# The trunk's MLP: up and down both as seven block products for eight, hidden values by way of DRAM

## The reference

```python
def mlp_sq_relu(hn, w_up, w_down):
    return jnp.square(jax.nn.relu(hn @ w_up)) @ w_down
...
        h = h + mlp_sq_relu(rmsnorm(h, norm_mlp[i]), w_up[i], w_down[i])
        gate = jax.nn.sigmoid(rmsnorm(h, norm_ple[i]) @ w_ple_gate[i])
        h = h + gate * (p[i] @ w_ple_proj[i])
```

## Time and profile before

| | us |
|---|---|
| median of 3 runs | 2668.34 |
| lowest, highest | 2668.11, 2674.18 |
| profiled execution, its own time | 2672.45 |
| its span, first to last instruction | 2670.8 |

### The profile page before, as it was taken

How to read it: one execution, slowest core, us unless ns; L and a number is a source line. 1 busy time by engine, 2 the same in 40 slices (tenths; PEclk the granted TensorE clock), 3 DMA queues, 4 the chain that set the end, 5 groups by cost and what they waited for, 6 DMA issues and landing times.

```text
span 2670.8 us, 33174 instructions
## 1 busy us (share of the span) xinstructions
PE 2598.1 (97%) x12228; PEld 2148.8 (80%) x12228; DVE 1693.7 (63%) x2448; ACT 1051.0 (39%) x1758; POOL 788.0 (30%) x671
## 2 busy tenths in 40 slices
PE   7999999899999999999999999989999999999996
PEld 6788888788888888888878888878888888888885
DVE  7667655645666766675665657664567766667555
ACT  6555433433333333334442333353333333333432
POOL 2000000023555555543120000002355554554213
PEclk9999999999999999999999999999999999999998
DMA  3000100121111111211221111012111111111121
GB/s 131 30 25 25 32 25 24 56 79 40 56 56 56 43 53 48 63 51 59 88 94 40 32 32 31 24 63 79 48 56 56 50 46 49 55 56 55 48 79 71
DMA packets 39531, 140.49 MB, mean 53 GB/s; under 512 B 4384, under 2 KB 4400, under 8 KB 39392
## 3 DMA queue, kind: packets, MB, share of 16 engines
q1 hardware_dynamic: 36448, 128.73, 15.6%
q0 software_dynamic: 2224, 7.54, 0.8%
q10 hardware_dynamic: 720, 2.36, 0.2%
HBM read 129.70 MB, written 8.91 MB: 52 GB/s over the span
## 4 chain that ended last, share of the span: by engine, by line
PE 73%; issue 16%; DVE 6%; ACT 4%; DMA 1%; DVEq 0%; POOL 0%; ACTq 0%; SPq 0%; POOLq 0%
PE gemm_ps L487 15%; PE gemm_ps L489 15%; PE gemm_ps L488 15%; PE s_ps L487 8%; PE s_ps L488 7%; PE s_ps L489 7%; PE to_ps L488 1%; PE to_ps L489 1%; PE to_ps L487 1%; PE to_ps L593 1%; ACT prob L1117 1%; DVE wlo L1462 1%; ACT whi L1031 1%; DVE prob L1584 0%; DVE h L2133 0%
## 5 line engine op out<-in xcount | busy, mean ns | idle before, releaser
L487 PE MATMUL gemm_ps<-b_hi,whi 128*128 128x512 f32 x1280 | 499.6, 390 | 0.0
L489 PE MATMUL gemm_ps<-b_hi,wlo 128*128 128x512 f32 x1280 | 498.0, 389 | 0.0
L488 PE MATMUL gemm_ps<-b_lo,whi 128*128 128x512 f32 x1280 | 497.9, 389 | 0.0
L487 PE MATMUL gemm_ps<-a_hi,whi 128*128 128x512 f32 x1024 | 424.3, 414 | 21.1 <-DVE a_lo L1471 10.8
L489 PE MATMUL gemm_ps<-a_hi,wlo 128*128 128x512 f32 x1024 | 402.6, 393 | 0.0
L488 PE MATMUL gemm_ps<-a_lo,whi 128*128 128x512 f32 x1024 | 401.3, 392 | 0.0
L1462 DVE TENSOR_TENSOR wlo<-wraw,whi 128x1024 fp32r<-128x1024 f32 x162 | 221.5, 1368 | 138.4 <-ACT whi L1031 137.8
L487 PE MATMUL s_ps<-hid_hi,whi 128*128 128x512 f32 x784 | 305.0, 389 | 0.0
L488 PE MATMUL s_ps<-hid_lo,whi 128*128 128x512 f32 x784 | 305.0, 389 | 0.0
L489 PE MATMUL s_ps<-hid_hi,wlo 128*128 128x512 f32 x784 | 305.0, 389 | 0.0
L487 PEld LDWEIGHTS gemm_ps<-b_hi,whi 128*128 128x128 f32 x1280 | 240.2, 188 | 50.8 <-issue 1.0
(11 more groups left out here) (267 smaller groups left out, 4417.4 us busy)
## 6 DMA issues: line engine op xcount, KB each, us to landing
wraw<-panels SPq DMA_DIRECT2D x162, 512.0 KB, 3.5
wraw<-pairs SPq DMA_DIRECT2D x56, 512.0 KB, 3.6
h<-x_t SPq DMA_DIRECT2D x11, 512.0 KB, 5.4
h_spill<-h POOLq DMA_DIRECT2D x8, 512.0 KB, 3.1
h<-h_spill SPq DMA_DIRECT2D x8, 512.0 KB, 4.4
out_t<-h SPq DMA_DIRECT2D x8, 512.0 KB, 2.8
h<-x_t ACTq DMA_DIRECT2D x4, 512.0 KB, 11.4
p_raw<-p_t POOLq DMA_DIRECT2D x2, 1024.0 KB, 6.0
```

What stands on the lines that cost most here:

```text
L487: nc.tensor.matmul(out, hi_w, hi_x, start=start, stop=False, skip_group_check=True)
L488: nc.tensor.matmul(out, hi_w, lo_x, start=False, stop=False, skip_group_check=True)
L489: return nc.tensor.matmul(out, lo_w, hi_x, start=False, stop=stop, skip_group_check=True)
```

## The change

The up projection is folded as well, and all of down. Each layer's MLP becomes a list of 34 turns of 7 blocks. Turns 0 to 15 are the up projection: turn n makes 256 hidden values by 1024 positions, as a 2x2 of 128x512 (a "sub", quarters B11, B12, B21, B22), each block product over 4 pieces of 128 inputs, so 12 matmuls. VectorE and ScalarE put the quarters together, scale, clamp and square them, and SP stores them in a DRAM tensor, four stores of 256 KB a turn. Turns 16 to 33 are down (`DOWN`: output pair q, first sub, number of subs): a block product over 4 subs is 12 matmuls, over 2 subs (turns 16, 17, 32, 33) 6. The subs are loaded back piece by piece, summed in place by GpSimd (4 sums a sub), split by ScalarE and VectorE, and kept for the two turns of each output group that use them; `taken_in(n, j)` says which block of which sub is split at position j of turn n.

Weights: a turn's raw pair is two loads of 512 KB (half that for two-piece turns); three of the four weight sums are made in place by GpSimd; split blocks stand in a ring of 4 places, made 3 blocks ahead (`AHEAD`). The four banks of PSUM alternate between two sets by turn. The sums u2 and p7 of down lie in zs, sumsq, zt and rstd, one pair of places for each q; before, u2 and m1 lay in zs and u3 apart. They are added to h at the end only: by GpSimd for q 0 to 2 (`tail_adds`), by VectorE for q 3.

The high parts of x for turn 0 are made while the output projection of the mixer still runs, together with the sums T1 to T4 of x on VectorE (`t_part`), and the low parts of T3 on GpSimd (`t3_lo`). The norm's matmuls before up follow block 1 of turn 0. The squares for the norm before the gate (`tail_square`, GpSimd's `tile_squares`) come after the high parts of h, the gate's next weight split and the copy of p; the norm's matmuls follow the gate's whole first panel. In an up turn VectorE has 9 steps for the quarters (5 read PSUM) and ScalarE 2 copies and 4 squares beside the 7 weight blocks; in a down turn VectorE has 7 reads of PSUM.

The diff, cut to what the text speaks of (removed lines are left out):

```diff
+SUBS = FF // (2 * P)
+UPS = SUBS
+DOWN = ([(2, 0, 2), (3, 0, 2)] +
+        [(q + 2 * h, 4 * c + 2 * h, 4) for c in range(4) for h in range(2) for q in range(2) if 4 * c + 2 * h < 14] +
+        [(2, 14, 2), (3, 14, 2)])
+TURNS = UPS + len(DOWN)
+LAST = TURNS - 1
...
+RING = 4
+AHEAD = 3
+RAMP = {(15, 2): [(0, 0)], (15, 3): [(0, 1), (0, 2)], (15, 4): [(0, 3)], (15, 5): [(0, 4), (0, 5)],
+        (15, 6): [(0, 6), (1, 0)], (16, 0): [(1, 1)], (16, 1): [(1, 2)], (16, 2): [(1, 3)], (16, 3): [(1, 4)],
+        (16, 4): [(1, 5)], (16, 5): [(1, 6)], (16, 6): [(2, 0)], (17, 0): [(2, 1)], (17, 1): [(2, 2)],
+        (17, 2): [(2, 3)], (17, 3): [(2, 4)], (17, 4): [(2, 5)], (17, 5): [(2, 6)]}
+def taken_in(n, j):
+    found = list(RAMP.get((n, j), []))
+    first = n - UPS + 1 if n % 2 else n - UPS
+    if n >= 17 and n % 2 and 4 <= first < SUBS and j:
+        found.append((first, j - 1))
+    if n >= 18 and n % 2 == 0 and 4 <= first < SUBS and j == 0:
+        found.append((first, BLOCKS - 1))
+    if n >= 17 and n % 2 and 2 <= first < SUBS and j == BLOCKS - 1:
+        found.append((first + 1, 0))
+    if n >= 18 and n % 2 == 0 and 2 <= first < SUBS and j < BLOCKS - 1:
+        found.append((first + 1, j + 1))
+    return found
...
+                def load_raw(n):
+                    if n == 0:
+                        sp.wait_ge(w_lo_ready, st["gate"])
+                    elif n == 1:
+                        sp.wait_ge(up_t3_ready, 4 * layer + 3)
+                        sp.wait_ge(up_t_ready, 16 * layer + UP_T.index(("T4", 2)) + 1)
+                    else:
+                        sp.wait_ge(blk_lo_ready, BLOCKS * (turn_of(layer, n) - 1))
...
+                def load_hidden(s, name):
...
+                    elif name == "B11":
+                        sp.wait_ge(hid_lo_ready, taken_at(layer, s - 1, X_BLOCK.index("T2")))
+                        sp.wait_ge(t_ready, t_made(layer, s - 1, "T4"))
+                    else:
+                        last = {"B12": "T3", "B22": "B22", "B21": "T4"}[name]
+                        sp.wait_ge(hid_lo_ready, taken_at(layer, s - 1, X_BLOCK.index(last)))
...
+                for n in range(UPS, TURNS):
+                    s = n - UPS + 2
+                    if n + 2 < TURNS:
+                        load_raw(n + 2)
+                    if s < SUBS:
+                        for name in ("B11", "B12", "B22", "B21"):
+                            load_hidden(s, name)
+                sp.wait_ge(blk_lo_ready, BLOCKS * turn_of(layer, LAST))
+                load_panels(st["gate"], 4 + KT)
...
+                def fold_turn(n):
+                    t, count = turn_of(layer, n), pieces_of(n)
+                    down = n >= UPS
+                    for j, (_, _, name, start) in enumerate(FOLD):
+                        out = BANKS[n % 2][name]
+                        pe.wait_ge(blk_lo_ready, BLOCKS * t + j + 1)
...
+                        if j == 0 and n >= 2:
+                            pe.wait_ge(fold_read, reads(layer, n - 1))
                         if j == 2:
+                            pe.wait_ge(fold_read if down else p_copied,
+                                       reads(layer, n) + 1 if down else 2 * (UPS * layer + n) + 1)
                         if j == 5:
+                            pe.wait_ge(fold_read if down else p_copied,
+                                       reads(layer, n) + 2 if down else 2 * (UPS * layer + n) + 2)
                         if j == 6:
+                            pe.wait_ge(fold_read, reads(layer, n) + (5 if down else 3))
+                        for i in range(count):
+                            x_hi, x_lo = input_block(n, j, i)
+                            last = product(out, blk(whi, layer, n, j)[:, i], blk(wlo, layer, n, j)[:, i], x_hi, x_lo,
+                                           start and i == 0, i == count - 1)
                         last.then_inc(fold_done, 1)
+                        if n == 0 and j == 1:
+                            norm_sums(st["norm"] + 1, to_ps)
+                for n in range(TURNS):
+                    fold_turn(n)
+                pe.wait_ge(fold_read, reads(layer, LAST) + 4)
+                for places in (range(KT - 2), range(KT - 2, KT)):
+                    for half in range(2):
+                        unit(Idx(st["gate"]), half, b_hi, b_lo, Idx(st["x_ple"]), places=places)
+                pe.wait_ge(fold_read, reads(layer, TURNS))
+                norm_sums(st["norm"] + 2, to_ps)
...
+                def x_sums(n, j):
+                    for s, i in taken_in(n, j):
+                        if i == 0:
+                            x_sum(s, "T1")
+                        if i == 1:
+                            x_sum(s, "T3")
+                            x_sum(s, "T2")
+                        if i == 2:
+                            x_sum(s, "T4")
...
+                def tail_adds(q):
+                    gp.wait_ge(fold_read, reads(layer, LAST - 3 + q + 1))
+                    done = 12 * layer + 4 * q
+                    u2, u3 = SUM_U2[q], SUM_P7[q]
+                    nc.gpsimd.tensor_tensor(u3, u3, u2, ALU.add).then_inc(tail_added, 1)
+                    nc.gpsimd.tensor_tensor(piece(2 * q, 1), piece(2 * q, 1), u2, ALU.add).then_inc(tail_added, 1)
+                    gp.wait_ge(tail_added, done + 1)
+                    nc.gpsimd.tensor_tensor(piece(2 * q + 1, 0), piece(2 * q + 1, 0), u3, ALU.add).then_inc(tail_added, 1)
+                    nc.gpsimd.tensor_tensor(piece(2 * q + 1, 1), piece(2 * q + 1, 1), u3, ALU.add).then_inc(tail_added, 1)
...
+                for n in range(TURNS):
+                    for j in range(BLOCKS):
+                        if n == LAST - 2 and j == 0:
+                            tail_adds(0)
+                        if n < LAST and j == 0:
+                            w_sum(n + 1, "S1")
+                        if n < LAST and j == 2:
+                            w_sum(n + 1, "S3")
+                        x_sums(n, j)
+                        if n < LAST and j == 5:
+                            w_sum(n + 1, "S2")
+                        if n < LAST and j == 6:
+                            w_sum(n + 1, "S4")
+                    if n == LAST - 2:
+                        gp.wait_ge(hid_lo_ready, BLOCKS * SUBS * (layer + 1))
+                        gp.dma_start(p_raw[:], p_t[layer].rearrange("k p n -> p k n")).then_inc(p_loaded, 16)
+                    if n >= LAST - 2 and n < LAST:
+                        tail_adds(n - (LAST - 2) + 1)
+                    if n == LAST - 1:
+                        for o in range(2):
+                            tile_squares(st["norm"] + 2, Idx(o), o == 0)
+                for o in range(2, KT):
+                    tile_squares(st["norm"] + 2, Idx(o), False)
...
+                def w_ahead(n, j):
+                    n, j = divmod(BLOCKS * n + j + AHEAD, BLOCKS)
+                    if n < TURNS:
+                        w_blk_hi(n, j)
...
+                        if n == LAST - 1 and j in (1, 3, 5):
+                            next_hi((j - 1) // 2, 0)
+                            next_hi((j - 1) // 2, 1)
+                        if n == LAST and j == 0:
+                            next_hi(3, 0)
+                            next_hi(3, 1)
+                        if n == LAST and j == 4:
+                            act.wait_ge(fold_done, BLOCKS * turn_of(layer, LAST) + 3)
+                            w_hi(Idx(st["gate"]))
+                for o in range(4, KT):
+                    for half in range(2):
+                        next_hi(o, half)
+                act.wait_ge(fold_done, BLOCKS * turn_of(layer, TURNS))
+                w_hi(Idx(st["gate"] + 1))
                 act.wait_ge(p_loaded, 16 * (layer + 1))
                 A(a_hi[:, 4:6], p_raw[:], ACT.Copy).then_inc(p_hi_ready, 1)
+                for o in range(KT):
+                    for half in range(2):
+                        tail_square(o, half)
+                norm_root_of(st["norm"] + 2, to_ps)
...
+                for n in range(TURNS):
+                    for j in range(BLOCKS):
+                        if j:
+                            out_of(n, j - 1)
+                        elif n:
+                            out_of(n - 1, BLOCKS - 1)
...
+                        for s, i in taken_in(n, j):
+                            hid_lo(s, i)
+                        w_ahead(n, j)
+                        if n == LAST - 1 and j in (1, 3, 5):
+                            split_of((j - 1) // 2, 0)
+                            split_of((j - 1) // 2, 1)
+                        if n == LAST and j == 0:
+                            split_of(3, 0)
+                            split_of(3, 1)
+                        if n == LAST and j == 4:
+                            w_lo(Idx(st["gate"]))
+                out_of(LAST, BLOCKS - 1)
+                for o in range(4, KT):
                     for half in range(2):
+                        split_of(o, half)
```

(1 more changed line is left out.)

903 lines of the change are left out of this document (495 added, 408 removed).

## The result

The change made the kernel slower: 2700.35 us median (2698.12 to 2701.68) against 2671.26 of the kernel before in the same session (2668.11 to 2675.55), ratio 1.011 with a 95% interval of 1.0097 to 1.0123. I had forecast 2648 with 2605 to 2700 as the range; the result lies just above the upper bound, and on the other side of no change. The profiled execution has a span of 2697.5 us, 26.7 more than before.

The account below looks back on a forecast made before the run. TensorE, busy 97%, was taken as the bound. The profiled 2672.5 us less 97.9 for matmuls plus 78 of added waits (39 a layer) gave 2652.6; the median, 4.1 lower, was forecast at 2648 us, range 2605 to 2700.

Parts of the forecast that it names:

- The gain: MLP: 432 fewer matmuls in all at 0.227 us each save 97.9 us.
- Up turns, 0: Turns 1 to 14: other engines' work and the hidden stores fit under 19.0 us a turn, cost 0.
- The norm, +18: Before the gate: TensorE waits about 16 us for the later squares; +18 us a layer (14 to 21).
- The middle, +3: Turns 18 to 30 of down: VectorE slightly late, 0.25 us a turn; +3 us a layer (0 to 44).
- Start, +1: Turn 0: last blocks of x form behind ready ones; +1 us a layer (0 to 4).
- 8 us of cover: Turn 0: three ready blocks give TensorE 8 us of work while the last blocks of x form.
- Ramp, +13 (3 to 21): Turns 15 to 17, into down: VectorE overfull, GpSimd interfering, a load 3 us late; +13 us a layer.
- the lead: Ramp into down: about 3 two-piece blocks made ahead, 4 us taken off the ramp's lateness.
- End, +4 (0 to 9): Turns 32 and 33: GpSimd's adds precede weight sums, VectorE carries six splits; +4 us a layer.
- R1: Turns 18 to 30: VectorE and GpSimd SBUF steps exclude each other fully, VectorE sets the pace; 2733 us, chance 0.22.
- R2: Ramp, start, middle and end: lateness absorbed by the three-block lead, only the norm remains; 2606 us, chance 0.20.
- R3: Hidden loads come late behind 1 MB pairs, 28 takes losing 1.5 us each; +42, 2690 us, chance 0.10.

Follow-up runs that it names:

- experiment 17: Changed kernel with B11/B12 loads earlier, norm matmuls behind the third per-layer product, first four residual tiles' splits after the last turn, product copies first: 2658.36 us, ratio 0.9946.
- experiment 2: Changed kernel with GpSimd's input sums T1 to T4 made on one column, leaving most of them out: 2670.06 us.
- experiment 7: Changed kernel with GpSimd's raw weight sums made on one column, except in the first layer's turn 0: 2669.42 us.
- Experiment 10: Changed kernel with eight of VectorE's low parts in turn 0 made twice, and GpSimd's twelve end additions a layer on one column: 2701.86 us.
- Experiment 11: Changed kernel with the splits of the first four residual tiles made after turn 33: 2695.83 us.
- experiment 5: Changed kernel with B11/B12 loaded ahead of the raw pair; before the gate, GpSimd sums squares of tiles 0 to 2, VectorE 3 to 7: 2675.96 us.
- experiment 14: On experiment 5, norm matmuls behind the third per-layer product and GpSimd's additions after turns 30 and 31 moved later: 2689.37 us, ratio 1.0062.

## Why the prediction was wrong

- **The gain**, 432 x 0.227 = 97.9 us, was right: the matmuls are gone, and the pace in up and middle is the old one. The Trainium skill's 215.7 ns for a step (TensorE: Matmul & The Clock Gate, "Wait — 56ns, not 53.3ns?") is not met after the change either; here it is 226.8.
- **Up turns, 0**: right, 0.0 in both layers. The hidden values' stores and the 112 GB/s cost nothing.
- **The norm, +18**: right in mechanism and in size, +16.4 and +17.5. But I took it for the change's price: TensorE had 22 us of products to do that need no norm, and experiment 17 gets 16.9 of the stretch back for 3.8 behind it.
- **The middle, +3**: 5.5 and 6.3 in turns 19 to 30, the mechanism as I had it. Experiments 2 and 7 each remove it nearly whole. Turn 18, which I counted here, belongs to the ramp's lateness.
- **Start, +1: the step that failed first.** "8 us of cover" counted TensorE's ready blocks, and never VectorE's work in that stretch: 18.3 us of own steps and some 9 of standing beside GpSimd. Experiment 10 shows each step paid in full, experiment 7 that without GpSimd's weight sums 3.8 of the 8.3 us are left. Measured 8.0 and 8.3, twice my upper bound: the one term that lies wholly outside its own range.
- **Ramp, +13 (3 to 21)**: 17.9 and 18.0 in turns 15 to 17, and 3.9 and 3.8 more in turn 18. The load behind the 1 MB pair was in it with 3 us and cost 4.2. GpSimd's interference was nearly right: in turns 16 and 17 VectorE was busy 32.9 us, 10.1 above the 22.8 that I had worked out for it alone, where I had added 7 to 9. Beside it GpSimd worked 20.9 us, so 0.48 for each us, within my "a third to a half". What failed is what I took off: 4 us for the lead, and what turn 18 "makes good". Turn 18 lost 3.9 us instead.
- **End, +4 (0 to 9)**: 8.2 and 9.4. The causes were named, at half their size. Experiment 11, without the splits, takes away all of turn 32's loss, and experiment 10, without most of the additions, all but 1.3.
- Sum: start +7.1, ramp with turn 18 +8.7, middle +2.9, end +4.8, norm -1.0 a layer make 22.5 us. Twice that, and 2 us of the per-layer products, turn my -20 into +27, as the spans show; the medians differ by 29.

Of the rivals, **R1** had the mechanism and the wrong place: not the 19 us of a middle turn but turn 0 and the ramp, where the same two engines have less time. By its own measure a middle turn fits while a GpSimd step costs VectorE under 0.78 us; the table gives (214.3 / 12 - 12.8) / 8 = 0.63, so the middle nearly fits. The Trainium skill (SBUF — State Buffer, "Who interferes with whom") says that two such instructions exclude each other; the rows agree (0.68 alone, 1.76 beside GpSimd), and experiments 2 and 7 give the frequency that was missing. **R2** fell: the lateness of start, ramp, middle and end was paid in each. **R3** held for 4 us a layer, in the ramp alone. My range ended at 2700 because I had put only 0.2 outside and given each bound of ramp, start and end a row of its own, though all three hang on VectorE and could miss together.

What stays open: how the 17.5 us of the ramp split up once the load is early. Four leave-outs gave prices that overlap, and half of the late input blocks can only be made after the stage before, since they lie in its storage; I did not try other storage. With the same load order the ramp lost 17.5 in some executions and 19.1 in others (experiments 5, 14 and 17), and I have no cause for that. Nor did I find a version of turn 0 that loses less and keeps all its sums.

## What to carry to other kernels

When a change makes TensorE's work shorter, add up every other engine's steps in each short stretch between stages, not only in the steady turn: the steady turns here lost 6 us a layer and the changes between stages, the norm among them, 54 and 57. Errors of such stretches are of one kind when one engine carries them all, so their bounds must be moved together. And before paying for a wait, look for work behind it that does not need it: moving four matmuls behind three products, with the copies of these products first in the in-order queues, some splits later and two loads earlier, turned 1.1% slower into 0.5% faster.
